# Feed-forward up projection of a hybrid decoder layer: 18 of 22 tile pairs as 2x2 block products with seven products for eight

## The reference, cut to what matters

```python
u = hn @ p['w_up']                       # (1032, 1024) x (1024, 2 * 2816)
y = p['conv_b']
for j in range(CONV_W):                  # 3 taps along the tokens
    y = y + p['conv_w'][j] * full[:, j:j + t]
a, g = jnp.split(y, 2, axis=-1)
x = x + g_f * ((jax.nn.silu(a) * g) @ p['w_down'])
```

## Time and profile before

| | us |
|---|---|
| median of 3 runs | 2366.75 |
| the runs | 2363.69 to 2370.45 |
| the profiled execution | 2366.48 |
| its span | 2364.7 |

### The profile page before, as it was taken

How to read it: one execution, slowest core, us unless ns; L and a number is a source line. 1 busy time by engine, 2 the same in 40 slices (tenths; PEclk the granted TensorE clock), 3 DMA queues, 4 the chain that set the end, 5 groups by cost and what they waited for, 6 DMA issues and landing times. The chain is left out here.

```text
span 2364.7 us, 46160 instructions
## 1 busy us (share of the span) xinstructions
PE 2299.8 (97%) x18425; PEld 2159.1 (91%) x18425; DVE 1478.7 (63%) x2667; ACT 1043.6 (44%) x2113; POOL 798.1 (34%) x1019
## 2 busy tenths in 40 slices
PE   7899999999999999999999999999999999999999
PEld 5788888888888888889887999998999999999999
DVE  5568686777767686866687424327455455545547
ACT  6465555656656555555333421125333323333331
POOL 1134252524343342524344224442323222223222
PEclk9999999999999999999999999999999999999999
DMA  7312122121213122121699613111111111111113
GB/s 276 99 41 87 55 63 84 56 100 52 95 46 101 40 77 67 56 91 37 240 347 344 237 45 117 45 54 34 54 45 45 45 48 51 46 45 45 54 45 97
DMA packets 75632, 213.19 MB, mean 90 GB/s; under 512 B 15770, under 2 KB 24602, under 8 KB 75418
## 3 DMA queue, kind: packets, MB, share of 16 engines
q1 hardware_dynamic: 74266, 206.05, 26.0%
q10 hardware_dynamic: 1152, 4.19, 0.4%
HBM read 175.49 MB, written 26.26 MB: 85 GB/s over the span
## 5 line engine op out<-in xcount | busy, mean ns | idle before, releaser
L170 PE MATMUL h_G<-xn_hi,h_w_hi 128*128 128x344 f32 x1392 | 466.9, 335 | 6.8 <-ACT h_d_oraw L869 5.0
L170 PE MATMUL h_G<-xn_hi,h_w_lo 128*128 128x344 f32 x1392 | 445.2, 320 | 0.0
L170 PE MATMUL h_G<-xn_lo,h_w_hi 128*128 128x344 f32 x1392 | 444.8, 320 | 0.0
L2355 POOL TENSOR_TENSOR h_w_lo<-h_w_raw,h_w_hi 128x1024 fp32r<-128x1024 f32 x87 | 215.5, 2477 | 495.3 <-DVE f_y L2554 208.4
L2291 PE MATMUL t_ps<-hn_hi,h_w_hi 128*128 128x344 f32 x1032 | 330.6, 320 | 1.5 <-issue 1.5
L2291 PE MATMUL t_ps<-hn_lo,h_w_hi 128*128 128x344 f32 x1032 | 330.0, 320 | 0.0
L2291 PE MATMUL t_ps<-hn_hi,h_w_lo 128*128 128x344 f32 x1032 | 329.9, 320 | 0.0
L1140 POOL TENSOR_TENSOR h_w_lo<-h_w_raw,h_w_hi 128x1024 fp32r<-128x1024 f32 x58 | 147.5, 2544 | 465.3 <-ACT h_w_hi L742 391.7
L170 PEld LDWEIGHTS h_G<-xn_hi,h_w_hi 128*128 128x128 f32 x1392 | 263.4, 189 | 43.6 <-issue 16.1
L170 PEld LDWEIGHTS h_G<-xn_lo,h_w_hi 128*128 128x128 f32 x1392 | 262.0, 188 | 4.5 <-issue 0.2
L170 PEld LDWEIGHTS h_G<-xn_hi,h_w_lo 128*128 128x128 f32 x1392 | 262.0, 188 | 0.0
(11 more groups left out here) (372 smaller groups left out, 5504.4 us busy)
## 6 DMA issues: line engine op xcount, KB each, us to landing
h_w_raw<-in_w_in SPq DMA_DIRECT2D x72, 512.0 KB, 3.7
h_w_raw<-in_w_ffn SPq DMA_DIRECT2D x66, 512.0 KB, 3.6
h_d_ada_w<-in_w_ada SPq DMA_DIRECT2D x32, 512.0 KB, 4.3
g_kp<-in_cache_k SPq DMA_DIRECT2D x32, 512.0 KB, 7.1
g_vp<-in_cache_v SPq DMA_DIRECT2D x32, 512.0 KB, 5.4
h_w_raw<-in_w_mix SPq DMA_DIRECT2D x24, 512.0 KB, 3.6
x<-in_xT SPq DMA_DIRECT2D x16, 516.0 KB, 7.7
n_ada_w<-in_w_ada SPq DMA_DIRECT2D x16, 512.0 KB, 12.5
```

What stands on the lines that cost most here:

```text
L170: ins = eng.matmul(out, w[:, k * P:(k + 1) * P], x[:, k, columns], start=(k == 0 and n == 0), stop=(k == n_k - 1 and n == 2))
L2355: pool.tensor_tensor(wlo[buf(n)][:, :], raw[n % 2][:, :], whi[buf(n)][:, :].bitcast(F32), ALU.subtract).then_inc(w_lo.sem, 1)
```

## The change

The first four f (`N_PLAIN`) stay as they were. For f = 4 to 21 the two up tiles (2 x 1024 weights) times the 1024 x 1032 input are read as 2x2 blocks: rows s, contraction in halves of 4 blocks, tokens in halves of 516. Seven products of quarter tiles (128x512 weights, called P1 to P7) replace eight. The inputs P5, P6 and P7 need are sums of input blocks, made once (`t_hi`, `t_lo`, and one block of the input overwritten in place); the weight blocks need four sums for each f (`block_sum` on DVE), and the outputs are put together by seven additions from PSUM on DVE, one operand or both of which stand in PSUM and SBUF. A product is 24 matmuls of 258 columns into a pair of banks. Weights, down weights too, move in quarters of 128x512, with a ring of three split quarters. The convolution is done in halves of the tokens. Down quarters (6 pieces) run between P7 and P4.

```diff
+N_PLAIN = 2 * GROUP
+QUARTER = KT * P // 2
+WIDE_HALF = NT // 2
+PIECE = WIDE_HALF // 2
+    for f in range(N_PLAIN, FT):
+        between = downs(g - 1, half) if g < N_GROUPS - 1 else downs(N_GROUPS - 2, 0)[half:half + 1]
+        order += [(n, f) for n in ("P1", "P2", "P6", "P5", "P7")] + between + [(n, f) for n in ("P4", "P3")]
+    return order + downs(N_GROUPS - 2, 1) + downs(N_GROUPS - 1, 0) + downs(N_GROUPS - 1, 1)
...
+def down_places():
+    for f in range(N_PLAIN, FT + 1):
+        gap = (QUARTERS[Q_AT["P7", f] + 1:Q_AT["P4", f]] if f < FT else DOWN_QUARTERS[-6:])
+        for n in range(len(gap) * D_PIECES):
+            pair = (min(f, FT - 1) - N_PLAIN + 1 + n % 4 // 2) % 4
+            places.append((2 * pair + n % 2, n))
...
         @block.tensor
+            def block_product(name, f):
+                for h in range(2):
+                    columns = slice(h * PIECE, (h + 1) * PIECE)
+                    for k in range(kh):
+                        for n, (wv, xv) in enumerate(((wp, xp), (wp, rp), (lp, xp))):
+                            ins = pe.matmul(ps[:, bank + h, 0:PIECE], wv[:, w], xv[:, k, columns], ...)
+                ins.then_inc(q_done.sem, 1)
+            def pieces_free(n):
+                if n > 0:
+                    pe.wait_ge(down_free.sem, down_free.at(PLAIN_DOWN + n, 0))
+            def down_quarter(q):
+                for r in range(2):
+                    for j in range(NP):
+                        n = D_PIECES * D_AT[q] + r * NP + j
+                        bank, at = DOWN_PLACES[n]
+                        pieces_free(n if at < 4 else n - 3)
+                        product(pe, ps[:, bank, 0:TH], wp[:, w], lp[:, w], *act_of(g), GROUP, cols(j)).then_inc(d_done.sem, 1)
+                block_product("P7", f)
+                pe.wait_ge(c11.sem, i + 1)
+                pe.wait_ge(u2.sem, i + 1)
+                for q in downs_between(f):
+                    down_quarter(q)
+                pe.wait_ge(u4.sem, i + 1)
+                pe.wait_ge(c22.sem, i + 1)
+                block_product("P4", f)
+                pe.wait_ge(u3.sem, i + 1)
+                block_product("P3", f)
...
         @block.gpsimd
+            def quarter_low(q):
+                quarter_free(pool, n - RING)
+                pool.wait_ge(q_hi.sem, n + 1)
+                pool.tensor_tensor(lo, src, hi.bitcast(F32), ALU.subtract).then_inc(q_lo.sem, 1)
...
         @block.vector
-                    ch(dve.tensor_tensor(t8[:, :], bank[:, n:TH], gain[:, 1:CS], ALU.mult))
+                    ch(dve.tensor_tensor(bank[:, n:TH], bank[:, n:TH], gain[:, 1:CS], ALU.mult))
                     ch.sync()
-                    ins = dve.tensor_tensor(xt[:, T:NT], xt[:, T:NT], t8[:, :], ALU.add)
+                    ins = dve.tensor_tensor(xt[:, T:NT], bank[:, n:TH], xt[:, T:NT], ALU.add)
+            for f in range(N_PLAIN, FT):
+                if f > N_PLAIN:
+                    right_up(f - 1)
+                    half_conv(f - 1, 1, 0)
+                cut(f - 1)
+                if f > N_PLAIN:
+                    half_conv(f - 1, 1, 1)
+                rest_sum(f)
+                gate_act(f - 1)
+                if f % 2 == 0:
+                    act_high(f - 1)
+                left_up(f)
+                if f == N_PLAIN:
+                    last_sum()
+                second_up(f)
+                if f + 1 < FT:
+                    sum_rows(f + 1)
+                third_up(f)
+                fourth_up(f)
+                right_gate(f)
+                between = downs_between(f)
+                take_quarter(between[0])
+                half_conv(f, 0, 1)
+                for q in between[1:]:
+                    take_quarter(q)
+                if f + 1 < FT:
+                    difference(f + 1)
+                    sum_less(f + 1)
+                left_gate(f)
+                half_conv(f, 0, 0)
+            right_up(f)
+            half_conv(f, 1, 0)
+            cut(f)
+            half_conv(f, 1, 1)
+            gate_act(f)
+            act_high(f)
+            for q in DOWN_QUARTERS[-6:]:
+                take_quarter(q)
```

More of the change, by code:

```diff
@@ new lines, in half_first_tap @@
+            def half_first_tap(f, s, side):
+                i, tile = f - N_PLAIN, 2 * f + s
+                w0, bias = (vec[:, at0 + r * n_cv + tile:at0 + r * n_cv + tile + 1] for r in (0, 3))
+                if s == 0 and side == 1:
+                    act.wait_ge(c22.sem, i + 1)
+                    act.wait_ge(act_f.sem, act_f.at(f, 0))
+                elif s == 0:
+                    act.wait_ge(c21.sem, i + 1)
+                elif side == 0:
+                    act.wait_ge(c11.sem, i + 1)
+                    act.wait_ge(act_lo.sem, act_lo.at(2 * f, 0))
+                else:
+                    act.wait_ge(c12.sem, i + 1)
+                part = conv_part(s, side)
+                act.activation(y[s][:, part], u[s][:, part], ACT.Identity, bias=bias, scale=w0).then_inc(half_tap.sem, 1)
@@ L2212, in _ @@
             silu(0)
-            for t in range(2, len(FFN_TILES)):
+            last = len(FFN_TILES) - 1
+            for t in range(2, last):
                 kind, n, s = FFN_TILES[t]
@@ L2436, in merge, with residual @@
                 copy(dve, mh[:, k, cols(j)], m[n % 2][:, :]).then_inc(m_hi.sem, 1)
-            def residual(bank, xt, gain, j, before, out):
+            def residual(bank, xt, gain, j, out):
                 a0, n = j * TH, (TH if j < NP - 1 else T - 2 * TH)
@@ L2573, in take @@
             def take(g, half, qs):
-                t = FFN_TILES.index(("down", g, half))
                 for q in qs:
@@ L2599, in _, with take_quarter @@
-            for g, half, qs in ((N_GROUPS - 2, 0, (2, 3)), (N_GROUPS - 2, 1, range(DOWN_OUT)), (N_GROUPS - 1, 0, range(DOWN_OUT)),
-                                (N_GROUPS - 1, 1, range(DOWN_OUT))):
-                take(g, half, qs)
+                        residual(bank, x[:, n_out, :], mod[:, 5 * KT + n_out, :], j, down_free)
+            def take_quarter(q):
+                kind, g, half, part = q
+                take(g, half, range(2 * part, 2 * part + 2))
+            dve.wait_ge(n_lo.sem, n_lo.at(NP * KT, 0))
```

510 lines of the change are left out of this document (455 added, 55 removed).

## The result

The changed kernel takes 2537.36 us (median of 4 runs, 2527.49 to 2540.54) against 2366.47 us of the kernel before beside it (4 runs): ratio 1.0714, 95% interval 1.0679 to 1.0748. It is slower by 171 us. The forecast of 2451 us had the direction and about half of the size; the time lies outside its range.

What follows compares the result with a forecast made beforehand. TensorE was taken as the bound, never waiting before the change. Gained 39.9 us of its work, lost 124.5 us in waits: net +84.6 on 2366.5, 2451 us; range 2385 to 2480 us, some 0.8.

Steps and rivals of the forecast that it cites:

- Products: Block products from f = 4 on: 121.6 ns per 258-column matmul, seven products 20.43 us, gaining 2.23 us per f, 40 us.
- TensorE's own work: TensorE's matmuls from f = 4 on, block products and downs without waits: 594.7 us, where it was 634.6.
- my low end: Fastest pace considered for a 258-column matmul of the block products, 0.112 us: gain 68 us instead of 40.
- Rival D: Pace of block-product matmuls doesn't fall with the columns, 168 x 0.1574: +171 us, 2538 us; chance 0.03.
- The waits: TensorE standing from f = 4 to the end, mostly before down pieces until DVE takes earlier ones: 124.5 us lost.
- the middle: f = 5 to 19: even f lose 6.4 us, odd 4.6, periods 38.2 and 36.4 against 34.0; 81.5 us lost.
- the pause at the end: At the tail the second down piece waits for DVE's first take, behind gate and half convolutions: 12.0 us.
- f = 4: Start of the changed part: `last_sum` stands before `second_up`, P6 waits behind POOL's low part of 2064 columns: 18.4 us lost.
- POOL against DVE: For each f, 14 us of POOL and 13 us of DVE exclude each other in 36, in queues that don't avoid each other.
- rival B: POOL and DVE seldom meet: f loses 3.8 us, period 35.6, +45 us, 2411 us; chance 0.23.
- rival E: Waits bring TensorE's clock down: one fall a period costing 1.5 us, +27 us, 2478 us; chance 0.09.
- Column sums before f = 4: Eight DVE sums of 2.3 us, 18 in all, over two f, hidden by 15 us of DVE idle time per f.

Runs made afterwards that it cites:

- without hand-backs: Changed kernel, but the first four down pieces of every gap wait only for takings of the gap before, not for all earlier pieces: 2403.9 us, ratio 1.0162.
- kernel with short low parts and no hand-backs: Kernel without hand-backs, with POOL making only 16 of 512 columns of each quarter's low part, the rest left out of the computation: 2350.8 us.

## Why the prediction was right and wrong

The profiled execution took 2535.0 us, 84 over the forecast. The changed part begins at 1736.90 (first matmul of P1); in the trace of the kernel before, f = 4 begins at 1726.04 and 635.2 us are left to the last start. From 1736.90 to the last start at 2529.79 are 792.9 us, for 719.2 of the forecast (594.7 + 124.5).

- *Products.* Right. 0.1195 us for a matmul of 258 columns lies between the 0.1216 taken and the 0.118 beside it; 18 x 168 x 0.0021 is 6 us less: at the measured paces TensorE's own work is 3024 x 0.1195 + 1440 x 0.1574 = 588 us. The 0.112 us of my low end is the pace of the earlier trace rows, 128 columns in plain float32; no run shows it for 258 columns in this format, and at it the gain would have been 69 us, not 68. Rival D's 2538 us is the measured number by chance: its pace of 0.1574 isn't there. The Trainium skill, "TensorE: Matmul & The Clock Gate", section "Back-to-back issue gap", gives 110.0 ns by its formula, which it states for an isolated matmul and not for a stream with weight loads; the measurement, 119.5, decides.
- *The waits.* Right in mechanism, place and size: 116.1 us for 124.5. The rows count idle time from the end of the last matmul's passage (0.32 us), the forecast from when the next could have started (0.157), so for each of the 85 waits some 0.16 us more belong to it: about 130 us in all, 5 over the forecast, an estimate from these rows. As the rows count, the middle has 84.2 us in the 15.6 periods between 1800 and 2440 us, 5.4 each for 5.5; the pause at the end is 12.3 for 12.0, and from 1738 to 1800 us, which is f = 4, it is 13.4 for 18.4.
- *POOL against DVE.* Right as a mechanism; rival B is out. Its worth was a little low (53 us for 42, without hand-backs).
- *The clock.* This is the step that failed, rival E: the sum had no term for it, and the rival gave a fall 1.5 us for each period, 27 us in all, and a chance of 0.09. PE was busy 792.9 - 116.1 = 677 us, 89 more than the 588 of its own work. Some 14 of these are the passages ahead of the waits; the other 75 are the half lost of the 151 us in which it streamed at the lower level. That is 4 us for each of 19 gaps, nearly three times my price. I had priced one short fall. In the trace the lower clock holds for 10 us, 2054.3 to 2064.5, and half of what TensorE streams in it is lost. The earlier trace rows had both numbers: 5 us at 0.71 behind a stretch that was busy 17.2 of 21. I took the waits' share of a whole period, 5 of 37 us, and concluded that it was small; but the waits of a gap stand together, 3.7 us in the 9 from 2050 to 2059.
- *Column sums before f = 4.* The second failed step. I let 15 us of idle time on DVE for each f hide them, and named 18 us as the price without cover. The cover is there on average, not where they stand: the convolution of f = 1 is behind them, POOL's low part of a weight tile behind that, TensorE behind that. The changed part begins 10.9 us later (1736.90 for 1726.04); the feed-forward itself had begun 2.5 us earlier. Taking the pause away gave back 5 us without hand-backs, and nothing clear of the spread with them.

The sum of it: 75 (clock) + 11 (sums) + 5 (waits) - 7 (TensorE's own work, 588 for 594.7) = 84 us, the whole miss within 1 us. The kernel with short low parts and no hand-backs agrees on the own work: 607.3 us from its first P1 to its last start, less 13.6 of waits, is 594, and it has 12 us of streaming at the lower clock, of which 6 are lost. The kernel without hand-backs was 24 us over its forecast for the same reasons: 11 us of clock, and the 11 us of the sums; some 2 us are left.

The Trainium skill, in the section "A second HAM failure mode: psum-queue depth-cycling" of the same page, tells of a kernel, in another format, in which short idle times of TensorE between groups of matmuls bring the clock down and up again. The traces agree: pieces of six matmuls (0.95 us of starts), waits of 0.7 to 2.1 us between them, and a fall in the gap shown; from 1700 us on the clock fell 19 times.

## What to carry to other kernels

A cluster of short waits on TensorE has a second price, as large as the first (the same matmuls kept TensorE busy 29 us longer with one hand-back in each of 19 gaps and 67 with three, for 31 and 61 us more of waits): price it by how long the lower clock holds in the nearest trace, and look at how dense the waits are where they stand, not over a period. A step put at nothing because an engine idles on average needs the idle time at its place, with what is queued behind it named down to TensorE. And a rotation of buffers should wait for the reader of its own buffer, not for the last reader: that one expression was 133 us, most of the way from a loss of 7% to the gain of 0.5% that is left with the queues rearranged.

## What the runs showed of the hardware that was not expected

- TensorE ran faster in total with 437 useless matmuls in its waits than without: 2493.0 us for 2537.4.
- In the gap shown a single wait of 2.07 us stood ahead of the fall of the clock, 0.9 us behind its end; the lower level then held for 10 us, although TensorE was busy without a break from 2058.47 on. From 1700 us on there were 34 us at the lower clock without hand-backs, 101 with one in a gap, 204 with three, 279 with five.
- A GpSimd instruction and a VectorE instruction of two SBUF operands hold each other up in both directions (the gate's product 1.73 us for 1.23, quarters on GpSimd 1.38 to 2.04 for 1.29), and a VectorE instruction of one operand is held too: 8 columns took 1.3 us on average for 0.28. Moving low parts to VectorE, which makes them in 0.69 us for 1.29, was, with a further new order, worth 30 us (2387.3 to 2356.8), although VectorE is the busier of the two; with low parts moved in odd pairs alone, and the orders changed too, it was 18 (2369.8). What the orders alone give of it wasn't tried.
